# Laying out every weight matrix on the host so that a one-megabyte load is 128 rows of 8 KB

## The chip, the cores and the metric

The kernel runs on one core of a Trainium2 chip. The metric is device time in microseconds of one execution; lower is better. The engines named below are PE (TensorE, matrix products; PEld is its weight load), ACT (ScalarE), DVE (VectorE), POOL (GpSimd) and SP (SyncE, which here only issues transfers). Sixteen DMA engines serve the core's transfer queues: in this kernel q1 carries what SP issues, q10 what ACT issues and q0 what POOL issues; q8 and q14 carry instructions.

## The reference, cut to what matters

One inference step of a two-layer encoder over 256 prompt tokens and 32 sample tokens (288 in all), width 1024, float32. Each layer is a mixer with three gated branches and then a feed-forward part, dense in layer 0 and top-2 of 8 experts in layer 1:

```
h = rmsnorm(x);  z = h @ w_in                       # 1024 x 7168
a = gelu(ua) * (W_s . rmsnorm(gelu(va)) + b_s);  b = attention(q, k, v);  c = gb * conv3(gc * cin)
x = x + (sum_b sigmoid(gate_b) * (branch_b @ w_branch_b)) @ w_out
layer 0:  x = x + (silu(h @ w1) * (h @ w3)) @ w2                      # 1024 x 2816, 2816 x 1024
layer 1:  x = x + sum over the 2 chosen experts of weight * swiglu_e(h)  # 8 experts, 1024 x 3584
```

At batch 1 nearly all traffic is weights. The change touches the nine weight arrays: w_in, w_branch, w_out, w1, w3, w2 and the experts' e_w1, e_w3, e_w2, which hold eight matrices each.

## The kernel before, in words

All activations stay in SBUF with features on the 128 partitions. Weights stream through a ring of four one-megabyte buffers (`ring`, 128 partitions x 2048 float32), which the expert phase widens to six with `spare0` and `spare1`. One load always brings one megabyte: 256 columns of a matrix with 1024 rows (`128x8x256`), 512 columns of a branch matrix with 512 rows (`128x4x512`), or 256 rows of a w2 matrix (`128x2x1024`). 109 such loads serve the two mixers and the dense part, 336 the eight expert jobs of 14 units with three matrices each.

SP issues them all, in the order of the stream, each as soon as its buffer is free (`load`, L539 to L546, and `expert_matrix`, L576 to L583). It waits for nothing else. A megabyte is then split for a precise product in a faster format: ACT rounds it in halves into `w_hi` (L734 in the mixers and the dense part, L874 in the experts), DVE subtracts to get `w_lo` (L987, L1316), and PE multiplies high by high, low by high and high by low (L1574 to L1576; L1664 to L1666 and L1690). Four buffers of each kind lie between them. A few matrices (v, va, the branches and w_out) are used by PE straight from the ring (L1451, L1538, L1551).

The start of the program is a chain. ACT issues x in two halves of 576 KB (L723), in rows of 1,152 bytes, while SP issues the first four weight matrices (v in two parts, q in two parts) and POOL issues `vec` and a broadcast table of attention biases (L686, L667). ACT squares x, four feature blocks for each half (L756), PE averages the squares (L1437), ACT takes the root (L765), DVE inverts it (L974) and scales x into h (L977), and then PE begins on v (L1451).

POOL has a chain of its own for the biases: load a table (L667), DVE extends it (L1040, L1042), store it as `bias_ext` in DRAM (L671) in rows of 16 KB, the same again for layer 1, then the layer's small inputs and bias tiles (L655 to L682). DVE takes its instructions in program order, so while it waits at L1040 nothing behind it runs: the copies of q and the `w_lo` halves of k.

Of the kernel before, what the change touches and what calls it, by code (L numbers as in the profile page):

```python
# [14 lines left out]
P = 128  # L15
D = 1024
# [22 lines left out]
UNIT = 256  # L39
KB = UNIT // P  # L40
# [17 lines left out]
def mixer_matrices(l):  # L58

    names = []  # L60
    for seg in ("v", "q", "k", "ua", "va", "cin", "gc", "gb"):
        names += [(seg, l, i) for i in range(2)]
    for h in range(2):
        for b in range(3):
            names += [("gate", l, 4 * b + 2 * h), ("gate", l, 4 * b + 2 * h + 1), ("branch", l, h, b)]
    names += [("out", l, i) for i in range(4)]
    return names


SEGMENT = {"ua": 0, "va": 1, "q": 2, "k": 3, "v": 4, "cin": 5, "gb": 6, "gc": 7, "gate": 8}  # L70
# [19 lines left out]
def slot_of(i):  # L90
    return i % RING
# [203 lines left out]
def encoder(nc, x_t, vecs, w_in, cache_k_t, cache_v, ws_t, bs, g_v, bias_rev, w_branch, w_out,  # L295
# [4 lines left out]
    with ctx:  # L300
        def sb(name, shape, dt=f32):
            return ctx.enter_context(nc.sbuf_tensor(name, shape, dt))

        def sem(name):
            return ctx.enter_context(nc.semaphore(name))
# [3 lines left out]
        ring = [sb(f"ring{i}", [P, 2048]) for i in range(RING)]  # L309
# [82 lines left out]
        expert_ring = ring + [spare0[:, :], spare1[:, 0:2048]]  # L392
        psum = ctx.enter_context(nc.psum_tensor("psum", [P, 8, 512], f32))

        slot_loaded = [sem(f"slot_loaded{i}") for i in range(EXPERT_RING)]
# [96 lines left out]
        def reader(name):  # L492
# [3 lines left out]
            if kind in ("a", "g", "y"):  # L496
                (_, u), j = at
                n, ready = {"a": (KB, silu_ready), "g": (KB, hid_ready), "y": (DT, sum_ready)}[kind]
                return ready, n * u + j + 1, 0, 0
# [34 lines left out]
        @block.sync  # L534
        def _(sp):

            lead_split = {STREAM[matrix]: c + 1 for c, (matrix, part) in enumerate(LEAD_ORDER) if part == 1}

            def load(i, dst, src):  # L539
                if i >= RING and i - RING in lead_split:  # L540

                    sp.wait_ge(split, lead_split[i - RING])
                elif i >= RING:

                    sp.wait_ge(bank_full, GROUP[LAST_USE[i - RING]][1] + 1)
                sp.dma_start(dst, src).then_inc(slot_loaded[slot_of(i)], 16)  # L546

            def tall(s, c=256):
                return ring[s][:, :].rearrange("p (k c) -> p k c", c=c)

            def mixer(l):
                for n in mixer_matrices(l):
                    i = STREAM[n]
                    s = slot_of(i)
                    if n[0] == "branch":
                        _, _, half, b = n
                        src = w_branch[l, b, :, half * 512:(half + 1) * 512]
                        load(i, tall(s, 512), src.rearrange("(k p) c -> p k c", p=P))
                    elif n[0] == "out":
                        load(i, tall(s), w_out[l, :, n[2] * 256:(n[2] + 1) * 256].rearrange("(k p) c -> p k c", p=P))  # L560
                    else:
                        c = SEGMENT[n[0]] * 512 + n[2] * 256
                        load(i, tall(s), w_in[l, :, c:c + 256].rearrange("(k p) c -> p k c", p=P))

            mixer(0)
            for u in range(DENSE_UNITS + 1):
                if u < DENSE_UNITS:
                    for k, w in enumerate((w1, w3)):
                        i = STREAM[("w1", u)] + k
                        load(i, tall(slot_of(i)), w[:, u * UNIT:(u + 1) * UNIT].rearrange("(k p) c -> p k c", p=P))  # L570
                if u:
                    i = STREAM[("w2", u - 1)]
                    load(i, tall(slot_of(i), D), w2[(u - 1) * UNIT:u * UNIT, :].rearrange("(k p) c -> p k c", p=P))
            mixer(1)


            def expert_matrix(e, m, unit):
                which = EXPERT_STREAM[m][0]
                s = m % EXPERT_RING
                dst = expert_ring[s][:, 0:2048].rearrange("p (k c) -> p k c", c=D if which == 2 else UNIT)  # L580
                cols = bass.ds(unit * UNIT, UNIT)
                src = e_w2[bass.ds(e, 1), cols, :] if which == 2 else (e_w1, e_w3)[which][bass.ds(e, 1), :, cols]
                sp.dma_start(dst, src.rearrange("o (k p) c -> p (o k) c", p=P)).then_inc(slot_loaded[s], 16)  # L583

            HEAD, TAIL = 2, 8

            def split_before(job, m, turn):


                at = m + JOB_MATRICES - len(EXPERT_STREAM) if m >= TAIL else m  # L590
                value = job * JOB_CHUNKS + (LEAD_CHUNKS + 2 * (at - EXPERT_RING + 1 + (0 if turn is None else EXPERT_RING)))
                sp.wait_ge(split, value if turn is None else turn * (2 * EXPERT_RING) + value)


            def other_matrices(job, e):
                for m in range(EXPERT_RING, TAIL):
                    split_before(job, m, None)
                    expert_matrix(e, m, EXPERT_STREAM[m][1])
                with sp.Fori(0, TURNS - 1) as i:
                    for m in range(HEAD, TAIL):  # L600
                        split_before(job, m, i)
                        expert_matrix(e, m, i * 2 + (2 + EXPERT_STREAM[m][1]))
                for m in range(TAIL, len(EXPERT_STREAM)):
                    split_before(job, m, None)
                    expert_matrix(e, m, EXPERT_STREAM[m][1])


            for m in range(EXPERT_RING):
                if m < RING:
                    last = max(i for i in range(LEAD) if slot_of(i) == m)  # L610
                    sp.wait_ge(bank_full, GROUP[LAST_USE[last]][1] + 1)
                else:

                    sp.wait_ge(a_ready, 2 * BT)
                    sp.wait_ge(b_ready, 2 * BT)
                expert_matrix(0, m, EXPERT_STREAM[m][1])
            sp.wait_ge(jobs_ready, 1)
            last_job = sp.value_load(job_count[0:1, 1:2], min_val=EXPERTS - 1, max_val=MAX_JOBS - 1)
            with sp.Fori(0, last_job) as job:
                e = sp.value_load(job_expert[0:1, bass.ds(job, 1)], min_val=0, max_val=EXPERTS - 1)  # L620
                other_matrices(job, e)
                e_next = sp.value_load(job_expert[0:1, bass.ds(job + 1, 1)], min_val=0, max_val=EXPERTS - 1)
                for m in range(EXPERT_RING):

                    sp.wait_ge(split, job * JOB_CHUNKS + (LEAD_CHUNKS + JOB_CHUNKS + 2 * (m - EXPERT_RING + 1)))
                    expert_matrix(e_next, m, EXPERT_STREAM[m][1])
            e = sp.value_load(job_expert[0:1, bass.ds(last_job, 1)], min_val=0, max_val=EXPERTS - 1)
            other_matrices(last_job, e)
# [90 lines left out]
        def _(act):  # L719
# [157 lines left out]
            def silu_unit(u):  # L877

                _, value, per_job, per_turn = reader(("ag", u))
                act.wait_ge(hid_ready, turns.value(value - 1, per_job, per_turn))  # L880
                act.wait_ge(chunk_used, turns.chunk(CHUNKS_IN[u], u in ("odd", "next")))
                nc.scalar.activation(e_silu, bank(("ag", u), P, UNIT), ACT.Silu).then_inc(silu_ready, 1)
# [526 lines left out]
        def _(pe):  # L1409
# [259 lines left out]
            def transpose_hidden(u):  # L1669
                take(("tr", u))  # L1670
                _, value, per_job, per_turn = reader(("ag", u))
                pe.wait_ge(hid_ready, turns.value(value, per_job, per_turn))
                for b in range(KB):
                    ins = nc.tensor.transpose(bank(("tr", u), P, 512)[:, b * P:(b + 1) * P], e_hid[:, b * P:(b + 1) * P], ident[:, :])
                give(ins)
# [112 lines left out]
```

## Time and profile before

| | |
|---|---|
| Time, median of 3 runs | 2054.56 us (2052.16 to 2054.73) |
| Span of the profiled execution, first to last instruction | 2049.7 us |
| PE, PEld busy | 1962.4 us (96%), 1786.8 us (87%) |
| DVE, ACT busy | 1369.6 us (67%), 1099.2 us (54%) |
| DMA packets, bytes | 367,653 packets, 486.25 MB, 237 GB/s over the span |
| Packets on q1 (weights) | 362,192, 466.64 MB, 67.9% of 16 engines |
| Rate in the full stretches of the expert phase | about 361 GB/s |

The profiled execution has no time of its own in the records beside its span; the median of the runs stands 4.9 us above the span, which is what lies before the first and after the last instruction. A packet in the profile is one contiguous piece that one DMA engine moves: a row of 256 floats is a packet of 1 KB. The "DMA" share is packet time over 16 engines, and can exceed 1 where packets overlap on an engine.

### The profile page before, as it was taken

The numbers are of one execution on the slowest core, as the hardware profiler recorded it, in microseconds if no ns is written. First come the engines' busy times: TensorE is split into PE (matmuls) and PEld (weight loads), VectorE is DVE, ScalarE is ACT, GpSimd is POOL, SyncE is SP. The second block draws the span as 40 slices with busy tenths as digits, with TensorE's granted clock in tenths as the row PEclk, the third lists the DMA queues.
The fourth block names the chain that finished last, engine by engine and source line by source line (L and its number), as shares of the span: only waits on it lengthen the run. The fifth ranks groups of instructions, "written<-read, shape, count | busy, mean of one in ns | idle before, by whom it ended". The sixth has DMA issues, their size and how long they took to land.

```text
span 2049.7 us, 35662 instructions
## 1 busy us (share of the span) xinstructions
PE 1962.4 (96%) x13034; PEld 1786.8 (87%) x13034; DVE 1369.6 (67%) x1839; ACT 1099.2 (54%) x1420; POOL 31.6 (2%) x60
## 2 busy tenths in 40 slices
PE   7999998999999999889999999999999999999996
PEld 5889987999888899679979889899899898898895
DVE  4382324666635532249969879789799698797895
ACT  3252213333434222137757767677677577676774
POOL 1101000000000000000000000000000000000000
PEclk9999999999999999979999999999999999999998
DMA  7764444455354235239969979889799699699892
GB/s 237 250 210 135 145 143 144 153 177 165 103 165 150 81 126 183 91 136 358 361 220 359 353 236 361 290 288 361 242 347 360 218 360 360 229 361 311 282 362 76
DMA packets 367653, 486.25 MB, mean 237 GB/s; under 512 B 8001, under 2 KB 326497, under 8 KB 367329
## 3 DMA queue, kind: packets, MB, share of 16 engines
q1 hardware_dynamic: 362192, 466.64, 67.9%
q0 software_dynamic: 4336, 17.46, 2.6%
q10 hardware_dynamic: 1056, 1.18, 0.2%
q8 instruction: 49, 0.80, 0.2%
q14 instruction: 20, 0.16, 0.0%
HBM read 477.38 MB, written 7.88 MB: 237 GB/s over the span
## 4 chain that ended last, share of the span: by engine, by line
issue 67%; PE 30%; DVE 1%; DMA 1%; ACT 0%; POOL 0%; ACTq 0%; DVEq 0%; POOLq 0%
PE psum L1574 7%; PE psum L1576 7%; PE psum L1575 7%; PE psum L1451 4%; PE psum L1538 2%; PE psum L1551 2%; DMA x<-in_x_t 1%; PE psum L1437 0%; DVE rstd L974 0%; DVE h L977 0%; PE psum L1511 0%; PE psum L1500 0%; DVE attn L1073 0%; DVE a_t L1149 0%; PE psum L1518 0%
## 5 line engine op out<-in xcount | busy, mean ns | idle before, releaser
L1316 DVE TENSOR_TENSOR w_lo<-ring,w_hi 128x1024 fp32r<-128x1024 f32 x448 | 543.4, 1224 | 99.7 <-ACT w_hi L874 83.4
L874 ACT ACTIVATE w_hi<-ring 128x1024 fp32r<-128x1024 f32 x448 | 475.5, 1064 | 141.7 <-PE psum L1666 106.0
L1664 PE MATMUL psum<-w_hi,h_hi 128*128 128x256 f32 x1792 | 519.7, 290 | 1.1 <-issue 0.3
L1666 PE MATMUL psum<-w_hi,h_lo 128*128 128x256 f32 x1792 | 510.3, 285 | 0.0
L1665 PE MATMUL psum<-w_lo,h_hi 128*128 128x256 f32 x1792 | 510.2, 285 | 0.0
L1664 PEld LDWEIGHTS psum<-w_hi,h_hi 128*128 128x128 f32 x1792 | 347.1, 194 | 9.8 <-issue 9.8
L1665 PEld LDWEIGHTS psum<-w_lo,h_hi 128*128 128x128 f32 x1792 | 347.2, 194 | 0.0
L1666 PEld LDWEIGHTS psum<-w_hi,h_lo 128*128 128x128 f32 x1792 | 347.0, 194 | 0.0
L1574 PE MATMUL psum<-h_hi,w_hi 128*128 128x288 f32 x1120 | 335.4, 299 | 7.5 <-DVE h_lo L993 6.6
L1575 PE MATMUL psum<-h_lo,w_hi 128*128 128x288 f32 x1120 | 331.6, 296 | 0.0
L1576 PE MATMUL psum<-h_hi,w_lo 128*128 128x288 f32 x1120 | 330.5, 295 | 0.0
L987 DVE TENSOR_TENSOR w_lo<-ring,w_hi 128x1024 fp32r<-128x1024 f32 x162 | 197.6, 1224 | 186.8 <-ACT w_hi L734 186.5
L1316 DVE TENSOR_TENSOR w_lo<-spare,w_hi 128x1024 fp32r<-128x1024 f32 x224 | 273.5, 1224 | 36.5 <-ACT w_hi L874 32.1
L874 ACT ACTIVATE w_hi<-spare 128x1024 fp32r<-128x1024 f32 x224 | 237.2, 1059 | 74.0 <-PE psum L1666 74.0
L734 ACT ACTIVATE w_hi<-ring 128x1024 fp32r<-128x1024 f32 x162 | 170.9, 1058 | 174.0 <-PE psum L1576 148.5
L1574 PEld LDWEIGHTS psum<-h_hi,w_hi 128*128 128x128 f32 x1120 | 211.1, 188 | 9.5 <-issue 8.9
L1576 PEld LDWEIGHTS psum<-h_hi,w_lo 128*128 128x128 f32 x1120 | 212.1, 189 | 0.0
L1575 PEld LDWEIGHTS psum<-h_lo,w_hi 128*128 128x128 f32 x1120 | 211.4, 189 | 0.5
L1690 PE MATMUL psum<-w_hi,hid_hi 128*128 128x512 f32 x448 | 140.3, 394 | 8.1 <-DVE hid_lo L1325 8.1
L1690 PE MATMUL psum<-w_hi,hid_lo 128*128 128x512 f32 x448 | 138.8, 391 | 0.0
L1690 PE MATMUL psum<-w_lo,hid_hi 128*128 128x512 f32 x448 | 138.7, 390 | 0.0
L769 ACT ACTIVATE gate<-psum 128x288 f32<-128x288 f32 x48 | 19.7, 410 | 165.1 <-PE psum L1576 164.6
(227 smaller groups left out, 2059.5 us busy)
## 6 DMA issues: line engine op xcount, KB each, us to landing
ring<-in_e_w SPq DMA_DIRECT2D x224, 1024.0 KB, 5.7
spare<-in_e_w SPq DMA_DIRECT2D x112, 1024.0 KB, 5.2
ring<-in_w_in SPq DMA_DIRECT2D x56, 1024.0 KB, 7.7
ring<-in_w SPq DMA_DIRECT2D x33, 1024.0 KB, 5.3
ring<-in_w_branch SPq DMA_DIRECT2D x12, 1024.0 KB, 9.8
ring<-in_w_out SPq DMA_DIRECT2D x8, 1024.0 KB, 6.4
bias_ext<-attn POOLq DMA_DIRECT2D x2, 2048.0 KB, 10.3
bias<-bias_ext POOLq DMA_DIRECT2D x2, 1536.0 KB, 14.4
```

The costliest lines, as they stand in the source:

```text
L734: nc.scalar.activation(dst, src, ACT.Copy).then_inc(rounded, 1)
L874: nc.scalar.activation(w_hi[buf][:, :], expert_ring[s][:, half * CHUNK_W:(half + 1) * CHUNK_W], ACT.Copy).then_inc(rounded, 1)
L987: nc.vector.tensor_tensor(low, src, high.bitcast(f32), ALU.subtract).then_inc(split, 1)
L1316: nc.vector.tensor_tensor(w_lo[buf][:, :], expert_ring[s][:, half * CHUNK_W:(half + 1) * CHUNK_W], w_hi[buf][:, :].bitcast(f32), ALU.subtr ...
L1451: ins = nc.tensor.matmul(bank((seg, l, hf, n), rows, 256), h[:, k, t0:t0 + rows], w[:, k, :], start=(k == 0), stop=(k == DT - 1))
L1574: nc.tensor.matmul(bank(name), high, src[0][:, k, :], start=(k == 0), stop=False)
L1575: nc.tensor.matmul(bank(name), high, src[1][:, k, :], start=False, stop=False)
L1576: ins = nc.tensor.matmul(bank(name), low, src[0][:, k, :], start=False, stop=(k == tiles - 1))
L1664: nc.tensor.matmul(p, he_hi[:, k, :], w_high, start=(k == 0), stop=False)
L1665: nc.tensor.matmul(p, he_hi[:, k, :], w_low, start=False, stop=False)
L1666: ins = nc.tensor.matmul(p, he_lo[:, k, :], w_high, start=False, stop=(k == DT - 1))
L1690: ins = nc.tensor.matmul(psum[:, 6 + hf, :], h_part[:, b, :], w_part[:, hf * 512:(hf + 1) * 512], start=False, stop=(last and h_part is hi ...
```

## The change

Every weight array is permuted on the host, before the launch, so that each megabyte that a load fetches is contiguous in DRAM and is stored partition by partition: 128 rows of 2048 floats, 8 KB each. The destination in SBUF is filled with exactly the same values at the same places. Loads by q1 are then one piece per partition (`128x2048`) instead of eight, four or two. The number of loads, their bytes, their order and the semaphores they wait for stay; so do all instructions of PE, ACT, DVE and POOL. x, the bias tables, caches and outputs keep their layouts.

```
-                        _, _, half, b = n
-                        src = w_branch[l, b, :, half * 512:(half + 1) * 512]
-                        load(i, tall(s, 512), src.rearrange("(k p) c -> p k c", p=P))
+                        src = w_branch[l, n[3], n[2]]
...
-                        c = SEGMENT[n[0]] * 512 + n[2] * 256
-                        load(i, tall(s), w_in[l, :, c:c + 256].rearrange("(k p) c -> p k c", p=P))
+                        src = w_in[l, 2 * SEGMENT[n[0]] + n[2]]
+                    load(i, ring[slot_of(i)][:, :], src)
...
-                dst = expert_ring[s][:, 0:2048].rearrange("p (k c) -> p k c", c=D if which == 2 else UNIT)
-                cols = bass.ds(unit * UNIT, UNIT)
-                src = e_w2[bass.ds(e, 1), cols, :] if which == 2 else (e_w1, e_w3)[which][bass.ds(e, 1), :, cols]
-                sp.dma_start(dst, src.rearrange("o (k p) c -> p (o k) c", p=P)).then_inc(slot_loaded[s], 16)
+                src = (e_w1, e_w3, e_w2)[which][bass.ds(e, 1), bass.ds(unit, 1), :, :]
+                sp.dma_start(expert_ring[s][:, 0:2048], src.rearrange("o u p c -> p (o u c)")).then_inc(slot_loaded[s], 16)
...
+    def columns_of(w, width=UNIT):
+        *lead, rows, cols = w.shape
+        w = w.reshape(*lead, rows // P, P, cols // width, width)
+        at = len(lead)
+        w = w.transpose(*range(at), at + 2, at + 1, at, at + 3)
+        return w.reshape(*lead, cols // width, P, 2048)
+    def rows_of(w):
+        *lead, rows, cols = w.shape
+        w = w.reshape(*lead, rows // UNIT, KB, P, cols)
+        at = len(lead)
+        return w.transpose(*range(at), at, at + 2, at + 1, at + 3).reshape(*lead, rows // UNIT, P, 2048)
...
-        "w_in": a["w_in"],
+        "w_in": columns_of(a["w_in"]),
```

## Rows read from the trace of the kernel before

**Rows 1.** Waits of PE, whole span: us in total, times, longest us.
```profile
PE psum L1674 <- DVE key_t L1321: 14.4, 8, 1.9
PE psum L1437 <- ACT rows L756: 10.6, 2, 9.5
```
**Rows 2.** Waits of ACT and of SP's queue, whole span, same columns.
```profile
ACT w_hi L874 <- PE psum L1666: 180.0, 336, 7.0
...
ACT w_hi L734 <- DMA ring<-in_w_in: 25.4, 9, 11.8
...
SPq L583 <- DVE w_lo L1316: 875.4, 330, 16.2
```
**Rows 3.** PE in the expert phase (timeline: start us, duration us, instruction).
```profile
943.79 0.28 PE L1665 MATMUL psum<-w_lo,h_hi 128*128 128x256 f32 x1
943.91 0.28 PE L1666 MATMUL psum<-w_hi,h_lo 128*128 128x256 f32 x1
```
**Rows 4.** Timeline from the start; in brackets the idle time before and its releaser.
```profile
7.62 1.28 ACT L756 ACT_TABLE_LOAD   x1 [7.62 <-DMA x<-in_x_t]
...
9.50 3.58 PE L1437 MATMUL psum<-rows,mean_w 128*128 128x288 f32 x8 [9.50 <-ACT rows L756]
13.70 1.44 ACT L756 ACTIVATE rows<-x 128x288 f32<-128x288 f32 x4 [3.34 <-DMA x<-in_x_t]
...
14.19 2.21 PE L1437 MATMUL psum<-rows,mean_w 128*128 128x288 f32 x8 [1.11 <-ACT rows L756]
...
19.74 22.79 PE L1451 MATMUL psum<-ring,h 128*128 128x256 f32 x96 [3.34 <-DVE h L977]
```
**Rows 5.** All DMA: 946 to 947 us (1 KB rows); 950 to 951 (4 KB); 0 to 4.
```profile
DMA packets 341, 0.35 MB, mean 347 GB/s; under 512 B 2, under 2 KB 341, under 8 KB 341
...
DMA packets 101, 0.41 MB, mean 414 GB/s; under 512 B 0, under 2 KB 0, under 8 KB 101
...
DMA packets 451, 0.47 MB, mean 117 GB/s; under 512 B 1, under 2 KB 451, under 8 KB 451
```
**Rows 6.** DMA queues from 7.6 to 10 us: packets, MB, share of 16 engines.
```profile
q0 software_dynamic: 135, 0.55, 63.5%
q10 hardware_dynamic: 148, 0.17, 24.3%
q1 hardware_dynamic: 148, 0.14, 19.9%
```
**Rows 7.** The same from 33 to 35 us: bias store (q0) beside weights (q1).
```profile
q0 software_dynamic: 48, 0.79, 92.3%
q1 hardware_dynamic: 48, 0.05, 6.9%
```
**Rows 8.** Queue q10, which carries x alone, over the whole span.
```profile
q10 hardware_dynamic: 1056, 1.18, 0.2%
```
**Rows 9.** PE by windows: from:to, us, busy (count), granted clock, DMA share, GB/s.
```profile
15.00:16.50 1.50, 1.40 (x6) 1.00 1.10 350
...
20.00:21.00 1.00, 1.00 (x3) 0.50 0.88 277
```
**Rows 10.** The v products of layer 1, in the chain that ended last.
```profile
556.99 21.39 PE psum L1451 x96
```
**Rows 11.** Timeline of PE and DVE around the second bias table.
```profile
42.47 0.40 PE L1574 MATMUL psum<-h_hi,w_hi 128*128 128x288 f32 x1
...
45.10 0.29 PE L1575 MATMUL psum<-h_lo,w_hi 128*128 128x288 f32 x1
...
48.13 1.22 DVE L1040 COPY attn<-attn 128x2040 f32<-128x2040 f32 x1 [16.77 <-DMA attn<-in_bias_rev]
...
49.77 1.22 DVE L987 TENSOR_TENSOR w_lo<-ring,w_hi 128x1024 fp32r<-128x1024 f32 x1
```
**Rows 12.** Bias tile load, issued at 64.7 us (us to landing), and its first use.
```profile
bias<-bias_ext POOLq DMA_DIRECT2D x1, 1536.0 KB, 16.2
...
103.24 0.29 DVE L1071 SCALAR_TENSOR_TENSOR attn<-psum,bias 128x128 f32<-128x128 f32 x1 [12.63 <-PE psum L1464]
```

More of the change, by code:

```diff
@@ L546, in load @@
                 sp.dma_start(dst, src).then_inc(slot_loaded[slot_of(i)], 16)
-            def tall(s, c=256):
-                return ring[s][:, :].rearrange("p (k c) -> p k c", c=c)
             def mixer(l):
@@ L553, in mixer @@
                     i = STREAM[n]
-                    s = slot_of(i)
                     if n[0] == "branch":
-                        _, _, half, b = n
-                        src = w_branch[l, b, :, half * 512:(half + 1) * 512]
-                        load(i, tall(s, 512), src.rearrange("(k p) c -> p k c", p=P))
+                        src = w_branch[l, n[3], n[2]]
                     elif n[0] == "out":
-                        load(i, tall(s), w_out[l, :, n[2] * 256:(n[2] + 1) * 256].rearrange("(k p) c -> p k c", p=P))
+                        src = w_out[l, n[2]]
                     else:
-                        c = SEGMENT[n[0]] * 512 + n[2] * 256
-                        load(i, tall(s), w_in[l, :, c:c + 256].rearrange("(k p) c -> p k c", p=P))
+                        src = w_in[l, 2 * SEGMENT[n[0]] + n[2]]
+                    load(i, ring[slot_of(i)][:, :], src)
             mixer(0)
@@ L569, in _ @@
                         i = STREAM[("w1", u)] + k
-                        load(i, tall(slot_of(i)), w[:, u * UNIT:(u + 1) * UNIT].rearrange("(k p) c -> p k c", p=P))
+                        load(i, ring[slot_of(i)][:, :], w[u])
                 if u:
                     i = STREAM[("w2", u - 1)]
-                    load(i, tall(slot_of(i), D), w2[(u - 1) * UNIT:u * UNIT, :].rearrange("(k p) c -> p k c", p=P))
+                    load(i, ring[slot_of(i)][:, :], w2[u - 1])
             mixer(1)
@@ L1763 @@
         "bias_rev": a["attn_rel_bias"][:, :, ::-1],
-        "w_branch": a["w_branch"],
-        "w_out": a["w_out"],
-        "w1": a["ffn_w1"][0], "w3": a["ffn_w3"][0], "w2": a["ffn_w2"][0],
+        "w_branch": columns_of(a["w_branch"], 512),
+        "w_out": columns_of(a["w_out"]),
+        "w1": columns_of(a["ffn_w1"][0]), "w3": columns_of(a["ffn_w3"][0]), "w2": rows_of(a["ffn_w2"][0]),
         "router": a["moe_router"][0], "router_b": a["moe_router_b"],
-        "e_w1": a["moe_w1"][0], "e_w3": a["moe_w3"][0], "e_w2": a["moe_w2"][0],
+        "e_w1": columns_of(a["moe_w1"][0]), "e_w3": columns_of(a["moe_w3"][0]), "e_w2": rows_of(a["moe_w2"][0]),
     }
```

## The prediction

> **What bounds the kernel now.** I read four views: the waits of PE, then those of ACT and SP, then the timeline of the first 60 us, then the DMA queues in short windows. PE is busy for 1962 of 2049.7 us, and none of its waits is for a transfer of weights: the two longest sums are for DVE inside an expert job and for the squares of x at the start (ACT L756) [rows 1]. In the expert phase ACT waits for PE to release a `w_hi` buffer, and SP waits 875 us for buffers to come free [rows 2]. So there the weights arrive before they are needed and PE sets the pace: 120 ns from one matmul of 256 columns to the next, without a break [rows 3]. That DMA moves 361 GB/s there is PE's rate of consumption, close to what the queue can do but not the limit. ACT's waits for weights come to 25.4 us in nine places, all in the mixers [rows 2]. PE runs without a gap through each of them, since up to four split halves lie ahead of it.
>
> One transfer is on the path: x. ACT waits for its first half until 7.62 us and for the second until 13.70, PE waits behind ACT, and PE's main work begins at 19.74 [rows 4]. From there on the program is PE's time and fixed chains.
>
> **What the change does to weight transfers.** A load keeps its megabyte, but 1,024 packets of 1 KB (or 512 of 2 KB, or 256 of 4 KB) become 128 of 8 KB. The 1 KB rows go at 347 GB/s, the 4 KB rows of w2 at 414 [rows 5]. No row shows 8 KB loads; I take 410 GB/s for them, near the 4 KB row. The bounds are 350 (no gain) and about 430 (as much again as a small step above 414). A faster load is worth nothing to PE where PE never waits for one, which is everywhere after 19.74 us. Cost and gain of all 445 loads in their steady state: 0. The cover is the depth of the ring; if the rate fell below the 361 GB/s that the experts consume, that cover would be gone (a rival, below).
>
> **What it does to x.** Three queues share the 16 DMA engines at the start, and the trace shows how. From 7.6 to 10 us q10 (x, packets of 1,152 B) and q1 (weights, 1 KB) pass 148 packets each and q0 (bias table, 4 KB) 135 [rows 6], though q0 moves over three times the bytes of either. From 33 to 35 us it is 48 packets of 16 KB against 48 of 1 KB, 0.79 MB against 0.05 [rows 7]. The engines take one packet from each queue in turn, whatever its size. The Trainium skill, DMA: Bandwidth & Descriptors, section "Queues, rings and completion order", says that an engine goes round its queues at packet granularity and drains a whole packet before it switches; the trace agrees, 48 to 48. By its figure of 9 to 17 descriptors in a packet the turn would be many rows long; by the 48 to 48 a turn here is one row, and I go by the rows.
>
> After the change each turn of x costs an 8 KB weight packet where it cost 1 KB. x has 1,056 packets [rows 8], 66 for each engine, 33 in each half (32 of data and one that signals). The first four weight loads give each engine 4 x 8 = 32 data packets and 4 signals, and they begin some 1.2 us before x, two or three packets' worth. So when x's 33rd packet passes, the 36 of the ring have passed too: the first half of x now comes only after all four weight matrices. The bias table on q0 (1.05 MB in 16 packets of 4 KB for each engine, and `vec`) also fits before it.
>
> Bytes that precede the landing of x's first half: 4.19 MB of weights + 0.59 of x + 1.09 on q0 = 5.87 MB. By 4.0 us 0.47 MB have moved [rows 5]; I keep that ramp. The other 5.40 MB at 410 GB/s take 13.2 us: the first half lands at 17.2 us (at 430, 16.6; at 350, 19.4). The second half is alone then, 0.59 MB at 350 GB/s, 1.7 us: 18.9.
>
> From there by the rows of before [rows 4]: ACT needs 1.28 us for its table load and then squares without pause, so the second half (18.9) is there before its turn (17.2 + 1.28 + 1.44 = 19.9). PE's first product starts 1.88 us after the landing (7.62 to 9.50), at 19.1. It has both groups of eight in one run, 3.58 + 2.21 = 5.8 us, and ends at 24.9, where it ended at 16.40. That is **+8.5 us** before the root. The early 7.62 landing hid the table load and the slow first group of products; now they stand behind the last data. If PE needed 3.58 us for both groups it would be +9.9. Root, inverse and first h take 3.3 us as before, to the first product of v.
>
> A credit is possible for PE's clock. The granted clock is 1.00 (2.4 GHz) before the pause and 0.50 (1.2 GHz) at 20 us after it [rows 9], and the v products take 22.79 us [rows 4]. In layer 1, after a similar pause but a long busy stretch, the same 96 take 21.39 [rows 10]. PE will have worked 5.8 us in one run before the pause instead of 2.2. The credit lies between 0 and 1.4 us; the start's own row is the nearer, so I take 0.5. **Sum for the start: +8.0 us.**
>
> **What else shares queues.** The bias chain on POOL competes with weights. At 33 us the store of 2.1 MB takes turns with the k load: eight rounds for each engine of 16 + 8 KB, 3.15 MB at 410 GB/s, 7.7 us to 40.7, where the store alone would take 5.1, to 38.1: 2.6 us later at most. The second table load has 16 rounds of 4 + 8 KB with some weights beside it, about 1 us more. DVE waits for it at L1040 until 48.13, and the `w_lo` half that PE wants next is made at 49.77 to 51.0 [rows 11]. PE starts its four ready halves at 42.47, 24 products each; the 19 up to 45.10 took 2.63 us, so 96 take 13 and it needs the fifth at about 55.3. Slack 4.2 us, added delay 3.6: hidden, barely. With everything shifted equally by the late start the slack stays. If it failed it would cost PE about 1 us once. The bias tiles land at 80.9 and are first used at 103.24 [rows 12]; 22 us cover them. Cost: 0, bound +1.
>
> **Total.** Span 2049.7 + 8.0 = 2057.7. The median of the runs stands 4.9 us above the span, so 2062.6 us, 0.39% slower; I say 2062.5. About 0.2% (4.1 us) is what can be told from no change.
>
> **Rivals.**
> - *8 KB rows go in smaller packets.* If each row were cut in two of 4 KB, ring and x would have 64 packets each; x's first half would land near 13 us and hide the table load again, but the second half would come with the end of the weights, near 18.9. Then the squares' products end 2.7 us after it as now (13.70 to 16.40), at 21.6, which is +5.2: 2059.8. For it: q1 has shown no packet above 4 KB. Against: q0 passes 16 KB in one [rows 7]. The Trainium skill, same page, section "SWDGE vs HWDGE vs iDMA", gives a packet as preferably at most 4,096 B; the trace disagrees for q0, and no row here tests q1. Chance 9%.
> - *x keeps its share (not slower).* If the engines' prefetch or the issue of the weights gives x as many bytes as now, it lands at 7.6 and 13.7 or up to 1.2 us earlier at the higher rate: 2053.4 to 2054.6, no change. It decides if q10 gets about a third of the bytes. For it: SP's later loads are issued some us after the first. Against: the equal counts [rows 6, 7]. Chance 11%.
> - *Weights pace the experts unseen (faster).* If the 361 GB/s were DMA's limit and PE's, 352 MB at 410 instead would save over 100 us: about 1940. Against: ACT and SP wait the other way [rows 2]. Chance 2%.
> - *Contiguous megabytes read slower.* Below 361 GB/s the experts become bound by transfers: at 347, 352 MB take 1015 us instead of 976, about +39, so 2100. Against: w2's loads are already one contiguous megabyte and are the fastest, 414 [rows 5]. Chance 4%.
>
> **Chances and range.** My forecast has 74%, with its own range 2058 to 2065.5: the landing of x from 16.6 to 19.4, the clock credit 0 to 1.4, the bias chain +1. Down to 2056 and up to 2066.5 it takes in the first rival and noise of the runs, and leaves out most of the second, the experts' two, and little else. Slower by over 0.2%: most of the forecast, the first rival and the last, 0.81. Within: the second rival and a small edge of the forecast, 0.16. Faster: 0.03.
>
> **What would show it.** Right: 128 data packets per load on q1, about 64,000 in all instead of 362,192; in the first 17 us q1 moves about eight times q10's bytes at equal counts; ACT's table load starts at 16.5 to 18 instead of 7.62 with hardly a wait before the second four squares; the first v product at 27 to 29 instead of 19.74; all later stages of equal length, ring landings shorter, PE's pitch 120 ns still. Wrong: a table load before 10 us, packets of 4 KB on q1, a change in the length of the expert phase, or a PE gap near 63 us from the bias chain.

## The result, and the profile after

The changed kernel takes 2066.93 us (2065.76 to 2067.38, 4 runs) against 2053.36 for the kernel before (2051.95 to 2054.73, 4 runs): ratio 1.0065, 95% interval 1.0051 to 1.0079. It is 13.6 us slower, where 8 were forecast; the time lies 0.4 us above the stated range. The profiled spans are 2065.2 and 2049.7 us, 15.5 apart. Two executions among the series below fell far out, one of the kernel before at 3271.99 us and one of `first8_old` at 8958.71, and the ratios leave them out. In `after` all lines behind the change stand 8 lower (L1437 is L1429, L1451 is L1443, L1574 is L1566, L987 is L979, L1040 is L1032).

The page of the changed kernel, all DMA and the weights' queue (packets, MB, share of 16 engines):
```profile
DMA packets 69540, 486.25 MB, mean 235 GB/s; under 512 B 8000, under 2 KB 9056, under 8 KB 12256
...
q1 hardware_dynamic: 64080, 466.64, 61.8%
```
The same bytes go in 64,080 packets on q1 instead of 362,192: 445 loads of 128 rows and 16 signals. The change does what it says, and an 8 KB row is one packet.

Its timeline from the start, to be read against [rows 4]:
```profile
0.79 1.04 ACTq L715 DMA_DIRECT2D x<-in_x_t  x2
...
18.65 1.28 ACT L748 ACT_TABLE_LOAD   x1 [18.65 <-DMA x<-in_x_t]
19.94 2.78 ACT L748 ACTIVATE rows<-x 128x288 f32<-128x288 f32 x8
...
20.53 5.97 PE L1429 MATMUL psum<-rows,mean_w 128*128 128x288 f32 x16 [20.53 <-ACT rows L748]
...
26.54 0.50 ACT L757 ACTIVATE rms<-psum,eps 128x288 f32<-128x288 f32 x1 [2.52 <-PE psum L1429]
...
29.83 23.08 PE L1443 MATMUL psum<-ring,h 128*128 128x256 f32 x96 [3.33 <-DVE h L969]
```
ACT's wait for the first half of x has grown from 7.62 to 18.65 us; the eight squares then run without a pause, and PE's 16 products take 5.97 us in one piece. PE begins on v at 29.83 instead of 19.74: +10.1 us. The queues of the changed kernel from 8 to 12 us, then from 18 to 20, are to be read against [rows 6]:
```profile
q1 hardware_dynamic: 117, 0.83, 52.8%
q0 software_dynamic: 116, 0.48, 38.5%
q10 hardware_dynamic: 119, 0.14, 10.9%
```
```profile
q10 hardware_dynamic: 430, 0.47, 66.0%
q1 hardware_dynamic: 3, 0.00, 0.1%
```
The counts are equal again, 117, 116 and 119, while q1 moves six times the bytes of x. In the second stretch the weights are done and x passes the rest alone.

The second loss is at q and k. DVE waits for the second bias table 24.3 us, and PE for the next `w_lo` half; the changed kernel's DVE, then its PE, to be read against [rows 11]:
```profile
65.74 1.22 DVE L1032 COPY attn<-attn 128x2040 f32<-128x2040 f32 x1 [24.29 <-DMA attn<-in_bias_rev]
...
67.38 1.22 DVE L979 TENSOR_TENSOR w_lo<-ring,w_hi 128x1024 fp32r<-128x1024 f32 x1
```
```profile
52.83 0.40 PE L1566 MATMUL psum<-h_hi,w_hi 128*128 128x288 f32 x1
...
68.65 0.61 PE L1566 MATMUL psum<-h_hi,w_hi 128*128 128x288 f32 x1 [2.75 <-DVE w_lo L979]
```
From PE's first q product to DVE's release it was 5.66 us before (42.47 to 48.13) and is 12.9 now. PE uses up its four halves and stands for 2.75 us. By windows of the changed kernel (from:to, us, PE busy, granted clock, DMA share, GB/s) this costs clock too:
```profile
66.00:68.00 2.00, 0.00 (x0) 1.00 0.00 0
68.00:69.00 1.00, 0.35 (x1) 0.82 0.61 262
69.00:70.00 1.00, 1.00 (x5) 0.50 1.25 524
70.00:71.00 1.00, 1.00 (x6) 0.50 0.62 262
71.00:72.00 1.00, 1.00 (x6) 0.50 1.25 524
72.00:73.00 1.00, 1.00 (x9) 0.97 1.18 344
```
After the stand the granted clock is 0.50 (1.2 GHz) for about three microseconds, and PE does 5 or 6 products in one microsecond where it does 9 or 10 at full clock.

The chain that ended last names the stages; these are its v and va products, its last norm product of layer 0 and its end in the changed kernel:
```profile
96.03 21.15 PE psum L1443 x96
...
338.79 3.89 PE psum L1429 x16
...
572.21 21.39 PE psum L1443 x96
...
2055.68 0.88 POOL out_y_t L701
```
Stage by stage, after minus before:

| Stage begins | before | after | difference |
|---|---|---|---|
| first v product | 19.74 | 29.83 | +10.1 |
| first q product | 42.47 | 52.83 | +10.4 |
| va, layer 0 | 81.12 | 96.03 | +14.9 |
| norm behind the mixer, layer 0 | 323.66 | 338.79 | +15.1 |
| v, layer 1 (before: [rows 10]) | 556.99 | 572.21 | +15.2 |
| last transfer | 2040.16 | 2055.68 | +15.5 |

All but 0.6 us of the loss has arisen by 96 us. The other 1,960 us, in which all but 12 of the 445 loads are issued, add those 0.6.

### The profile page after: what moved, and what is told of

Read it like the earlier page. It is cut to its first block, busy times and chain, and to the rows that moved or that the text cites. A ratio compares the mean times of both kernels' runs of the same rounds, so it can differ in the third digit from the quotient of the medians.

```text
span 2065.2 us, 35614 instructions
## 1 busy us (share of the span) xinstructions
PE 1965.2 (95%) x13034; PEld 1789.2 (87%) x13034; DVE 1369.5 (66%) x1839; ACT 1099.5 (53%) x1420; POOL 31.7 (2%) x60
## 3 DMA queue, kind: packets, MB, share of 16 engines
q1 hardware_dynamic: 64080, 466.64, 61.8%
## 4 chain that ended last, share of the span: by engine, by line
issue 67%; PE 28%; DVE 2%; DMA 2%; ACT 0%; POOL 0%; ACTq 0%; DVEq 0%; POOLq 0%
PE psum L1566 7%; PE psum L1568 7%; PE psum L1567 7%; PE psum L1443 3%; PE psum L1530 2%; PE psum L1543 2%; DMA x<-in_x_t 1%; PE psum L1429 1%; DMA attn<-in_bias_rev 1%; DMA bias_ext<-attn 1%; DVE w_lo L979 1%; DVE h L969 0%; DVE rstd L966 0%; DVE h_lo L985 0%; PE psum L1503 0%
## 5 line engine op out<-in xcount | busy, mean ns | idle before, releaser
L1566 PE MATMUL psum<-h_hi,w_hi 128*128 128x288 f32 x1120 | 336.4, 300 | 10.3 <-DVE h_lo L985 6.6
L979 DVE TENSOR_TENSOR w_lo<-ring,w_hi 128x1024 fp32r<-128x1024 f32 x162 | 197.7, 1224 | 180.1 <-ACT w_hi L726 179.8
L1566 PEld LDWEIGHTS psum<-h_hi,w_hi 128*128 128x128 f32 x1120 | 211.7, 189 | 12.5 <-issue 8.9
```

The costliest lines, as they stand in the source:

```text
L979: nc.vector.tensor_tensor(low, src, high.bitcast(f32), ALU.subtract).then_inc(split, 1)
L1566: nc.tensor.matmul(bank(name), high, src[0][:, k, :], start=(k == 0), stop=False)
```

## The experiments

Two theories stood against each other; the letters are those of the expectations. T: engines take one packet from each queue in turn, so 8 KB weight packets hold up x at the start (10 us) and the bias chain at q/k (4.5 us), and nothing else is changed. S: the new layout costs a little on each load. Each run names its own further rivals.

**Parts of the change alone.** In `first4_new` only the first four loads have the new layout; in `rest_new` all but these; in `experts_new` only the experts' arrays.
```
 first4_new (on before):  if i < RING: load(i, ring[s][:, :], w_first[i])       # w_first: v and q, new layout
 rest_new (on after):     if i < RING: load(i, ..., w_first[:, c:c + 256].rearrange("(k p) c -> p k c", p=P))
 experts_new (on before): the new expert_matrix, columns_of(e_w1), columns_of(e_w3), rows_of(e_w2)
```


> Layout of before, except that the first four weight loads (v and q of layer 0) are 128 rows of 8 KB. Theory T (queues take one packet each in turn, so x waits behind these four loads): ACT's table load starts near 18.6 us as after the change, the first v product near 29.8, and since all later loads have 1 KB rows the second bias table arrives some 5.7 us after PE starts on q as in before, so PE has no 2.75 us wait there. About +10.4 us against before: 2063.8. Rival S (the new layout costs a little on every load, all over the program): 4 of 445 loads cost nothing, 2053.4.

Measured: 2063.85 us, ratio 1.0055 (1.0038 to 1.0072), +10.5. ACT in `first4_new`:
```profile
18.39 1.28 ACT L759 ACT_TABLE_LOAD   x1 [18.39 <-DMA x<-in_x_t]
```
Four of 445 loads carry three quarters of the loss. S is out, and the cost at the start is shown.

> The changed kernel, except that its first four weight loads keep the old layout with 1 KB rows. Theory T: x lands at 7.6 and 13.7 us as in before, first v product at 19.7; the bias chain still competes with 8 KB rows of k and ua, so PE's wait of 2.75 us for w_lo and the slow clock behind it stay, some 4.7 us: 2058.1. Rival B (PE's wait at q and k is only a consequence of the late x, not of the packet size in the bias chain): 2053.4. Rival S (all loads cost a little): 2066 or so.

Measured: 2058.12 us, ratio 1.0021 (1.0012 to 1.0031), +4.8: the median is T's. But its ten runs spread from 2053.5 to 2061.9, and the profiled one (2055.2) had no `w_lo` wait: the 96 v products took 24.44 us, so SP issued the three weight loads behind v only at 44.5, and POOL's table load, issued 4.5 us ahead of them, had the engines nearly to itself:
```profile
40.03 0.91 POOL L664 DMA_DIRECT2D attn<-in_bias_rev  x1 [7.53 <-DMA bias_ext<-attn]
...
46.32 1.22 DVE L1037 COPY attn<-attn 128x2040 f32<-128x2040 f32 x1 [14.67 <-DMA attn<-in_bias_rev]
```
That is 6.3 us from issue to use. So the second cost is a race: it is paid when the weight loads come together with the table load, as in `after` (table 52.66, first load 52.94). Which of the two cases the slower runs were is not recorded; that it explains their spread is likely, not shown. Rival B, that the wait only follows from a late x, is not settled by this profile; `after_xrows` below settles it.

> Only the experts' three arrays in the new layout (336 of 445 loads), all of layer 0 and the mixers as before. Theory T: no PE wait in the expert phase is for a transfer, so 2053.4, within 1.5 us; loads' time to landing changes and PE's pace does not. Rival S: most of the cost, +10 us or more. Rival F (transfers pace the experts): faster by tens of us.

Measured: 2053.35 us, ratio 1.0002 (0.9993 to 1.0012). 336 of the loads change nothing: S and F are out.

**Which rows hold up x.** The four first loads in pieces of 4 KB and 2 KB, all else as before.
```
+ load(i, tall(s, PIECE), w_first[i].rearrange("k p c -> p k c"))     # PIECE = 1024 or 512 floats
```


> Layout of before, except that the first four weight loads are pieces of 4 KB (two for each partition). Theory T, one packet a turn: x needs 33 turns for each half, now of 4,096 + 1,152 B and for a while 4,096 B of the bias table: halves land near 13.1 and 19 us, first v product near 25: about 2058.6. Rival M (only packets above 4 KB hold others up): x as in before, 7.6 and 13.7. Rival A (any long packet lets the ring finish first): halves as with 8 KB, 18.4 and 20.

> The same with pieces of 2 KB (four for each partition). Theory T: halves of x land near 9.2 and 14.8 us, first v product near 20.8: about 2054.5. Rivals M and A as for 4 KB.

Measured, one run each: 2060.55 and 2054.58 us. ACT's two waits for x in `first4_4k`, then in `first4_2k`:
```profile
13.58 1.28 ACT L760 ACT_TABLE_LOAD   x1 [13.58 <-DMA x<-in_x_t]
20.33 1.44 ACT L760 ACTIVATE rows<-x 128x288 f32<-128x288 f32 x4 [4.02 <-DMA x<-in_x_t]
```
```profile
9.85 1.28 ACT L760 ACT_TABLE_LOAD   x1 [9.85 <-DMA x<-in_x_t]
16.40 1.44 ACT L760 ACTIVATE rows<-x 128x288 f32<-128x288 f32 x4 [3.81 <-DMA x<-in_x_t]
```
With rows of 1, 2, 4 and 8 KB beside it, the first half of x lands at 7.6, 9.9, 13.6 and 18.4 us (expected 9.2 and 13.1 for the middle two), the second at 13.7, 16.4 and 20.3. M and A are out; the size of the rival's packet sets the price, in steps as the turns count them. The second halves came 1.3 to 1.6 us later than worked out.

**Remedies for x.** Fewer, longer packets for x, or x ahead of the weights.
```
 after_xrows:  x_t laid out as (2, P, 4 * TOK); dma_start(x[:, 4 * k:4 * k + 4, :], x_t[k].rearrange("p (q t) -> p q t", t=TOK))
 after_hold:   + sp.wait_ge(x_in[1], 16)      # ahead of mixer(0)
```


> The changed kernel with x laid out on the host so that each of its two halves is 128 rows of 4,608 B instead of 512 rows of 1,152 B. Theory T: x needs 8 turns for each half instead of 32; its first half lands near 7 us, its second near 11, both earlier than in before (7.6 and 13.7), so the first v product is at 16.5 to 18 us instead of 29.8; the cost in the bias chain stays (about 4.7 us). About 2066.9 - 12.5 = 2054.5. Rival Q (x is held up by bytes queued ahead of it, not by turns): no change, 2066.9.

Measured: 2055.29 us, ratio 1.0012 (1.0003 to 1.0022), 11.6 under `after`. x's halves landed at 7.66 and 12.80, the first v product was at 18.85; I had expected 16.5 to 18, since I had not multiplied the nine turns by the 8 + 4.6 KB of each. Q is out: the same bytes of weights were queued ahead. The wait for `w_lo` is still there, 2.9 us, though PE begins on v earlier than in before: B is out.

> The changed kernel with one wait more: SP issues its first weight load only when both halves of x have landed. Theory T: x has the engines to itself from 3.2 us, its halves land near 4.9 and 6.7 us; ACT's table load is then at 4.9 and the first v product near 15.9 instead of 29.8; v's first part lands near 12, before its use. Bias chain as in after. 2066.9 - 13.9 = 2053.0. Rival L (v now lands too late and PE waits for it instead): first v product at 20 or later, 2057 or more.

Measured: 2053.37 us, ratio 1.0002 (0.9992 to 1.0012), 13.6 under `after`. PE in `after_hold`, both v's start and the wait at k:
```profile
16.49 11.78 PE L1444 MATMUL psum<-ring,h 128*128 128x256 f32 x52 [3.33 <-DVE h L970]
```
```profile
PE psum L1567 <- DVE w_lo L980: 3.2, 1, 3.2
```
The matrix of v is no bound (L is out), and what is left at k is the second cost.

**The bias chain.** `after_reorder` moves DVE's extension of the second table behind the copies of q; `next4_old` gives 1 KB rows only to loads 5 to 8 (k and ua), which run beside the store and the table.
```
-                    for layer in range(2):
-                        extend_rows(layer)
+                    extend_rows(0)
...
+                    if l == 0 and s == "q":
+                        extend_rows(1)
 next4_old:               if RING <= i < 2 * RING: load(i, ..., w_first[:, c:c + 256].rearrange(...))
```


> The changed kernel; only DVE's order differs: the extension of the second bias table (L1032) stands behind the copies of q and the first four w_lo halves of k instead of ahead of them. Theory T (the table load is late because its packets take turns with 8 KB weight packets, and DVE's in-order wait passes this on to PE): the 2.75 us wait of PE at q/k and the slow clock behind it go, first v product still at 29.8: 2066.9 - 4.7 = 2062.2. Rival C (the time lost there is the ring's own: k's load is late): no change, 2066.9.

Measured: 2063.26 us, ratio 1.0049 (1.0032 to 1.0066), 3.7 under `after`; no `w_lo` wait, first v product at 30.26. C is out: once DVE does not stand at the table, PE does not stand for k.

> The changed kernel, except that weight loads 5 to 8 (k in two parts, ua in two parts), those that run beside the bias store and the second bias table, keep 1 KB rows. Theory T: start as in after (first v product near 29.8 us); the table load takes 7 us as in before instead of 13 and PE has no 2.8 us wait for w_lo: 2066.9 - 4.7 = 2062.2. Rival O (the table is late because POOL issues it later in the new order of events, not because of 8 KB rows): wait stays, 2066.9.

Measured: 2064.84 us, ratio 1.0054 (1.0037 to 1.0071), 2.1 under `after`. There is no `w_lo` wait; DVE's wait for the table in `next4_old` and the v products of that execution:
```profile
57.52 1.22 DVE L1037 COPY attn<-attn 128x2040 f32<-128x2040 f32 x1 [14.87 <-DMA attn<-in_bias_rev]
```
```profile
31.03 24.20 PE psum L1448 x96
```
The table needed 6.5 us from its issue at 50.99 instead of 13.1, but this execution does not test the race. v took 24.2 us instead of 23.1, SP issued the three loads only at 55.26, 4.3 us behind the table, and the table had the engines nearly to itself, as in the profile of `rest_new`. O is not settled by it.

`first4_new` is the better witness. It starts late as `after` does, its v products take 23.08 us as there, and its loads of k and ua have 1 KB rows. Its table, issued at 50.45 with the loads at 52.29, 52.70 and 53.63, released DVE at 58.08, after 7.6 us, without a `w_lo` wait. Over all profiles with the old DVE order in which the loads came within 3 us of the table, the six with 1 KB rows in k and ua (`before`, `experts_new`, `first4_new`, `first4_4k`, `first4_2k`, `first8_old`) had a table load of 7.0 to 7.9 us and no `w_lo` wait; the three with 8 KB rows (`after`, `after_xrows`, `after_hold`) had one of 10.6 to 13.2 us and a wait of 2.8 to 3.2.

In time the two remedies give 3.7 and 2.1 us, and `first4_new` against `after` 3.1. With four runs each, the 95% intervals reach some 3 us to either side and overlap, so the times alone do not size the second cost; `rest_new`, with ten runs, puts it at 2.5 to 6.4 us, and the stage table at 4.5.

**All of it together.** `first8_old`: the first eight loads with 1 KB rows, the other 437 with 8 KB. `after_best` and `before_best`: x in long rows, the hold and the new DVE order, on either layout.

> The changed kernel, except that its first eight weight loads keep 1 KB rows; the other 437 have 8 KB rows. Theory T: all of the cost sits in those eight loads, so first v product at 19.7 us, no w_lo wait, 2053.4 within 1.5 us. Rival S (a small cost on every load besides): 2055.5 or more. Rival P (a gain on the later loads, hidden so far by the start): under 2051.

Measured: 2052.87 us, ratio 0.9996 (0.9986 to 1.0006); the first v product was at 19.98, and there was no `w_lo` wait. Eight loads carry the whole loss; 437 of them in the new layout are worth nothing, neither way (S and P are out).

> The changed kernel with all three remedies: x in rows of 4,608 B, SP's first loads held until x has landed, and the second bias table's extension moved behind the copies of q on DVE. Theory T: first v product near 15.8 us, no PE wait at q/k: 2066.9 - 13.9 - 4.7 = 2048.3, about 5 us under before. Rival L (v or q land too late behind the hold): 2052 or more.

> The same three edits on the kernel before, weights in the old layout. Theory T: the layout of weights matters only where a transfer is waited for, and there is none left: within 1 us of after_best, about 2048.5. Rival P (8 KB rows do pay once nothing collides): slower than after_best by 2 us or more, for the first v matrix lands later. Rival N (8 KB rows still cost): faster than after_best.

Measured: 2049.75 us, ratio 0.9980 (0.9971 to 0.9989), and 2049.37, ratio 0.9983 (0.9974 to 0.9992). They are 3.2 and 3.6 us under the kernel before of the same series (2052.92), 1 to 1.5 us less than expected: the starts of v (16.69 and 17.04) came one microsecond later, and in the profiled executions v took long again, in `after_best` and in `before_best`:
```profile
16.69 24.14 PE psum L1444 x96
```
```profile
17.04 24.26 PE psum L1452 x96
```
Without collisions the layouts are equal within the intervals of 2 us to either side; P's loss of 2 us or more and L's late matrices are not seen, and a small N cannot be told. The gain comes from x in long rows ahead of the weights and from DVE's order, and it needs no new layout of weights.

## Why the prediction was wrong

For the start the direction, the mechanism and the place were right: one packet a turn, x behind all four weight matrices, nothing in the steady state. That supplies 10 of the 13.6 us. What was missed is a second place, which the prediction had looked at and priced at nothing. Term by term, in us of the profiled span:

| Term | forecast | measured |
|---|---|---|
| first half of x lands | 17.2 | 18.65 |
| landing to end of the squares' products | 7.7 | 7.85 |
| PE's clock in v | -0.5 | +0.3 |
| bias chain | 0, bound +1 | +4.5 |
| everything later | 0 | +0.6 |
| sum | +8.0 | +15.5 |

*The failed step* is "Slack 4.2 us, added delay 3.6: hidden, barely. [...] If it failed it would cost PE about 1 us once. [...] Cost: 0, bound +1." The slack was right: PE wanted its fifth half 13.1 us after its first q product. The delay was 7.2 us, not 3.6. The store came 1.5 us later (10.63 against 9.1 to landing, where I had up to 2.6), but the table load took 13.1 us instead of 7.1, where I had put "about 1 us more". I counted "some weights beside it", though three loads are released together when v is done. The text's own rule gives more: sixteen rounds of 4 + 8 KB on 16 engines are 3.15 MB, 7.7 us at 410 GB/s. DMA queues of the kernel before from 43 to 47 us, then of the changed one from 53 to 57 and from 57 to 65:
```profile
q0 software_dynamic: 234, 0.95, 92.6%
q1 hardware_dynamic: 12, 0.01, 0.9%
```
```profile
q1 hardware_dynamic: 125, 1.00, 73.8%
q0 software_dynamic: 3, 0.01, 0.8%
```
```profile
q1 hardware_dynamic: 270, 1.97, 62.7%
q0 software_dynamic: 264, 1.04, 38.9%
```
From 57 us on the two queues take turns, 264 packets against 270, and the table's 256 data packets need 7.8 us where they needed 4.9: +2.9, what the rule gives. But from 53 to 57 it is 3 against 125, and that is no taking of turns. The table's first packet passed 4.3 us after its issue instead of 1.6: +2.7 us that the rule of turns does not explain.

In the fourteen profiles this second delay goes with the order of issue. Where the weight loads were issued 1.5 us or more behind the table, its first packet came 1.6 to 1.8 us after its issue (ten profiles); where they came between 2.8 us ahead of it and 0.3 us behind it, 4.1 to 4.3 us (`after`, `after_xrows`, `after_hold`, `after_reorder`). The row size alone does not make it: at the start of the program, POOL's `vec`, issued at 2.35 us behind SP's first loads, had its first packet at 6.46 us in before and 6.43 in the changed kernel. In `after` the 8 KB rows brought the loads close to the table by holding up the store by 1.5 us. Why a load issued second has to wait is open. SP's queue at that point, before and after:
```profile
42.98 5.08 SPq L546 DMA_DIRECT2D ring<-in_w_in  x2
```
```profile
52.94 1.30 SPq L546 DMA_DIRECT2D ring<-in_w_in  x3
```
With 1,024 rows a load, SP was busy handing over the second and third load until 48.06, as the table landed (48.13); with 128 rows all three are handed over in 1.3 us. The sign that I had named for being wrong here, a gap of PE near 63 us, came at 65.9.

Where I priced the cover as gone, I priced only the stand of PE, not the slow clock behind it (0.50 for three microseconds, about 1.8 us), although the row of PE's clock at 20 us lay before me.

*x's landing*: I took 410 GB/s throughout. The changed kernel moved 0.60 MB by 4 us and 1.64 from 4 to 8 (411 GB/s), but 360 from 8 to 12 and 363 from 12 to 14, while three queues took turns; the row for three queues in before, 0.86 MB in 2.4 us or 359 GB/s [rows 6], would have said so. A bound of 350 was in the text, for one term.

*The clock*: the credit rested on a longer run of PE before its pause. The 96 products of v took 23.08 us after 5.97 us of work, 22.79 after 2.21. But one execution of each does not decide it: with the same late start they took 21.39 us in `after_reorder` and 24.20 in `next4_old`. The credit was drawn from a difference that equal code shows by itself.

*The base*: I added 4.9 us, the median less the span, to reach a time. In every run with both numbers the time is 1.7 to 1.8 us above the span (2066.95 and 2065.2). The profiled execution of before was thus some 2 us faster than its median, and the difference of spans overstates the loss by about that.

*The range*: its own terms do not give the forecast's own range of 2058 to 2065.5. A landing at 19.4, no credit and the bound of 1 us make 2066.3, and the lower ends make 2061.1. The bias chain's 4.5 us lie outside both.

The rivals: smaller packets and an undisturbed x are refuted by the profile of the changed kernel (64,080 packets on q1, x at 18.65 us); a gain or a loss in the experts by `experts_new`.

## What to carry to other kernels

In this kernel longer rows cost and gained nothing on the loads that nobody waits for, but each is a longer turn for every other queue: look for short-packet transfers that are waited for while bulk loads run, count their packets, and multiply them by the rival's packet size. Issue what the first instruction needs ahead of the bulk, or give it equally long rows. When a cover is "hidden, barely", count what is released together at that moment and in which order, and price its failure with the slow clock behind the stand.

## What the runs showed of the hardware that I had not expected

In these two kernels the spread of equal runs goes with the mean granted clock. In the 22 runs of `after_best` and `before_best`, those with a mean clock of 0.982 or 0.981 took 2046.4 to 2048.1 us, those with 0.980 took 2048.5 to 2049.9, and those with 0.979 took 2051.3 to 2051.9. In the profiles it shows at the v products behind the norms, where PE has just paused: the same 96 took 21.39 us, 22.8 to 23.1 or 24.1 to 24.4 in layer 0, and in layer 1, where all kernels run the same instructions, 21.39 or 23.0 to 23.1. That is up to 3 us in one stage, nearly as much as the second cost, so a difference of 2 or 3 us between two profiles must be traced to its wait. What decides which is open.

Weight loads of the experts landed later with 8 KB rows though nothing else changed (median us from issue to landing), in before and in `experts_new`:
```profile
ring<-in_e_w SPq DMA_DIRECT2D x224, 1024.0 KB, 5.7
```
```profile
ring<-in_e_w SPq DMA_DIRECT2D x224, 1024.0 KB, 7.0
```
No engine loses time by it (`experts_new` takes 2053.35 us). It is not a lower rate as such: with q1 nearly alone, 8 KB rows moved 428 GB/s from 55 to 57 us in `after`. Why the loads land later was not tried.
